# Two hybrid layers and two mixer layers on one core: the context keys of layers 0 and 1 are normalised in another order, their low parts are made by GpSimd, and the first query head is begun tile by tile

## The chip, the cores and the metric

The kernel runs on one core of a Trainium2 chip. The metric is the device time of one execution in microseconds (us); lower is better. The time before is the median of three runs.

## The reference, cut to what matters

Four layers follow each other on 512 positions of 1024 channels. The change lies in the first two (`l` = 0 and 1), in the latent attention of each:

```python
q = jnp.einsum("bsr,rk->bsk", rms_norm(q_lat, q_norm_g), w_uq)      # 384 -> 8 heads x (64 + 32)
q_nope, q_pe = jnp.split(q, [QK_NOPE], axis=-1)
q_pe = apply_rope(q_pe, cos, sin)
kv = jnp.einsum("bsr,rk->bsk", rms_norm(kv_lat, kv_norm_g), w_ukv)  # 256 -> 8 heads x (64 + 64)
k_nope, v = jnp.split(kv, [QK_NOPE], axis=-1)
```

`rms_norm(x, g)` is `x * rsqrt(mean(x*x) + eps) * g`. The latents `q_lat` (384 channels) and `kv_lat` (256 channels) and `k_rope` (32) are chunks of one projection of the layer's input. Causal attention over `qf`, `kf`, `v`, two convolution branches, a gated merge and a layer norm follow; then two more layers of another kind, which the change does not touch.

## The kernel before

**Numbers.** Every product of activations and weights is made of three matmuls: each operand is split into a high part (a rounded copy, `fp32r`) and a low part (the operand minus its high part), and `product` (L2034 to L2039) issues high x high (L2037), high x low (L2038) and low x high (L2039). A head of queries needs three tiles of 128 channels, so nine matmuls of 128x512; a chunk of the input projection needs eight tiles, so 24.

**Weights.** They come as blocks of 128x1024 through three slots. SyncE loads a block as soon as GpSimd has made the low part of the block three before it; ScalarE makes the high part (`split_to`, L483, or L480 for the two key and value blocks, which it also rearranges), for which the block must have landed and TensorE must have released the block three before it; GpSimd makes the low part in four pieces of 256 columns (`low_part`, L420, or `key_value_low`, L430). A chunk waits for the low part of each of its blocks. SyncE also loads pieces of `w_ada`, which VectorE multiplies up (`products`, L1239 and L1243).

**The stage around the change.** Block numbers here are those of layer 0; layer 1 has the same with 87 added. Blocks 6, 7 and 8 hold the query weights (24 tiles, three to a head), 9 and 10 the key and value weights, 11 is the first of the next stage. Block 10 takes the slot of block 7, which TensorE releases within head 5. Each engine runs its own program in order:

- TensorE: chunk of `k_rope`; sums of the squares of `kv_lat` by matmuls with ones (L2107); query heads 0 to 7 into four banks in turn; four key chunks (two heads each); four value chunks; then the first chunk of the next stage and the first attention scores. Head `h` from 4 on waits until ScalarE has taken (`qf`, L576) and VectorE has rotated head `h - 4`. The key chunks wait for the low parts `knL` of the normalised latent.
- VectorE: normalised query latent and its low parts (L1429, L1432, L1179); rotation of `k_rope`; for each head the rotation (L1448, L1449, L1451); behind head 1 the reciprocal of the key and value root (L1462) and the scaling of `kv_lat` (L1465, two tiles); behind head 3 the low parts `knL` (L1179, two tiles); behind every odd head a few `products`.
- ScalarE: high parts of the query latent (L606); high part of weight block 8; the root of the key and value sum (`kv_std`, L611); then per head the copy out of its bank (L576), with the high parts `knH` (L617) and the high part of block 9 behind head 2, block 10 behind head 5 and block 11 behind head 7; then eight copies of keys (L622) and four of values.
- GpSimd: low parts of the blocks in order: 8, then 9 and 10 (L430), then 11.

The lines that the change takes apart are these:

```python
pe.wait_ge(dve_done, Dn(l, "qnL", 2))           # TensorE, before head 0
pe.wait_ge(dve_done, Dn(l, "knL", 1))           # TensorE, before the first key chunk
```

Of the kernel before, what the change touches and what calls it, by code (L numbers as in the profile page):

```python
# [20 lines left out]
F32 = mybir.dt.float32  # L21
F32R = mybir.dt.float32r
I32 = mybir.dt.int32
ACT = mybir.ActivationFunctionType
ALU = mybir.AluOpType
# [4 lines left out]
S = 512  # L30
# [4 lines left out]
HEADS, NOPE, ROPE, VH = 8, 64, 32, 64  # L35
QL, KVL = 384, 256
# [19 lines left out]
POOL_PIECE = 256  # L56
RING = 3
Q_BANK = (4, 5, 0, 1)
# [55 lines left out]
def program(nc, io, known):  # L114

    ctx = ExitStack()
    with ctx:
# [8 lines left out]
        def sem(name):  # L126
            return ctx.enter_context(nc.semaphore(name))
# [18 lines left out]
        q_lat, kv_lat = at(R_L, [128, 3, S]), at(R_L + 3 * T, [128, 2, S])  # L146
        qnH, qnL = at(R_L + 5 * T, [128, 3, S], F32R), at(R_L + 8 * T, [128, 3, S], F32R)
        knH, knL = at(R_L + 11 * T, [128, 2, S], F32R), at(R_L + 13 * T, [128, 2, S], F32R)
# [7 lines left out]
        tmp = [at(R_T + T * i, [128, S]) for i in range(5)]  # L156
# [103 lines left out]
        s_park = nc.dram_tensor("s_park", [MH, 4, 128, SEQ], F32, kind="Internal").ap()  # L260
        ctx_landed, dft_landed, mask_landed = sem("ctx_landed"), sem("dft_landed"), sem("mask_landed")
        xm_parked, xc_parked = ([sem(f"{n}_parked{i}") for i in range(2)] for n in ("xm", "xc"))
        s_parked, xc_low = sem("s_parked"), sem("xc_low")
        xm_back, xc_back, s_back = sem("xm_back"), sem("xc_back"), sem("s_back")


# [51 lines left out]
        def B_UQ(l): return PER_LAYER * l + 6  # L318
# [93 lines left out]
        @block.gpsimd  # L412
        def _(pool):

            def low_part(b, slot):

                pool.wait_ge(weights_hi, b + 1)
                for i in range(0, BLK, POOL_PIECE):
                    part = slice(i, i + POOL_PIECE)
                    low = pool.tensor_tensor(w_lo[slot][:, part], w_raw[slot][:, part], w_hi[slot][:, part].bitcast(F32), ALU.subtract)  # L420
                low.then_inc(weights_lo, 1)

            def key_value_low(b):

                pool.wait_ge(weights_hi, b + 1)
                for n in range(4):
                    t, i = n // 2, 4 * (n % 2)
                    part = slice(POOL_PIECE * n, POOL_PIECE * (n + 1))
                    low, high = (w[b % RING][:, part].rearrange("p (h c) -> p h c", h=4) for w in (w_lo, w_hi))
                    low = pool.tensor_tensor(low, by_head(w_raw[b % RING])[:, i:i + 4, t, :], high.bitcast(F32), ALU.subtract)  # L430
                low.then_inc(weights_lo, 1)

            first = 0
            for l in range(L1):
                with pool.Fori(first, B_UKV(l) // RING) as i:
                    for r in range(RING):
                        low_part(i * RING + r, r)
                for b in UKV_BLOCKS[2 * l:2 * l + 2]:
                    key_value_low(b)
                low_part(b + 1, (b + 1) % RING)  # L440
                first = B_UKV(l) // RING + 1
            with pool.Fori(first, BASE_A // RING) as i:
                for r in range(RING):
                    low_part(i * RING + r, r)

            for b in range(BASE_A, BASE_B):
                low_part(b, b % RING)
                for h in range(MH):  # L450
                    for c in range(NC):
                        if b == ((AB["gates", 1] if h == 1 else AB["x", h, 3],) * 2 + (AB["q", h, 0], AB["q", h, 1]) if h else (AB["x", 1, 0], AB["x", 1, 1], AB["q", 0, 0], AB["q", 0, 1]))[c]:
                            pool.wait_ge(act_done, A("xcH", h, c))
                            for i in range(0, SEQ, POOL_PIECE):
                                part = slice(i, i + POOL_PIECE)
                                low = pool.tensor_tensor(xcL[:, c, part], c_acc[c % 2][:, part], xcH[:, c, part].bitcast(F32), ALU.subtract)  # L456
                            low.then_inc(xc_low, 1)
            with pool.Fori(BASE_B // RING, NBLOCKS // RING) as i:
                for r in range(RING):
                    low_part(i * RING + r, r)  # L460
# [3 lines left out]
        def _(act):  # L464
# [93 lines left out]
            for l in range(L1):  # L558
# [45 lines left out]
                for j in range(3):  # L604
                    act.wait_ge(dve_done, Dn(l, "qn", j))
                    act.activation(qnH[:, j, :], q_lat[:, j, :], ACT.Copy).then_inc(act_done, a(l, "qnH", j))  # L606

                act.wait_ge(pe_done, P(l, "k_rope"))
                split_to(B_KR(l) + 1 + RING)
                act.wait_ge(pe_done, P(l, "kv_sq", 1))  # L610
                act.activation(tmp[0][:], banks[2][:], ACT.Sqrt, bias=eps_rms[:], scale=1.0 / KVL).then_inc(act_done, a(l, "kv_std"))  # L611
                for h in range(HEADS):
                    evac(qf[0:NOPE, h, :], banks[Q_BANK[h % 4]][0:NOPE, :], (l, "q", h), None)
                    if h == 2:
                        for j in range(2):
                            act.wait_ge(dve_done, Dn(l, "kn", j))
                            act.activation(knH[:, j, :], kv_lat[:, j, :], ACT.Copy).then_inc(act_done, a(l, "knH", j))  # L617
                    if h in (2, 5, 7):
                        split_to(B_UQ(l) + RING + (h + 1) * 3 // 8)
                for h in range(HEADS):  # L620
                    act.wait_ge(pe_done, P(l, "k", h // 2))
                    act.activation(kf[0:NOPE, h, :], banks[KV_BANK[h // 2 % 2]][NOPE * (h % 2):NOPE * (h % 2 + 1), :], ACT.Copy)\  # L622
                        .then_inc(act_done, a(l, "k", h))
                for t in range(4):
                    evac(v_tok[:, t, :], banks[KV_BANK[t % 2]][:], (l, "v", t), None)
                split_to(B_UKV(l) + 2 + RING)
# [539 lines left out]
        def _(dve):  # L1166
# [4 lines left out]
            def wa(*label):  # L1171
                dve.wait_ge(act_done, A(*label))
# [4 lines left out]
            def low(dst, src, hi, *label):  # L1177

                dve.tensor_tensor(dst, src, hi.bitcast(F32), ALU.subtract).then_inc(dve_done, d(*label))  # L1179
# [199 lines left out]
            for l in range(L1):  # L1379
# [76 lines left out]
                for h in range(HEADS):  # L1456
                    wp(l, "q", h)
                    rotate(qf[64:96, h, :], banks[Q_BANK[h % 4]], l, "q_pe", h)
                    if h == 1:

                        wa(l, "kv_std")
                        dve.reciprocal(tmp[0][:], tmp[0][:]).then_inc(dve_done, d())  # L1462
                        wd()
                        for j in range(2):
                            dve.scalar_tensor_tensor(kv_lat[:, j, :], kv_lat[:, j, :], V("kv_norm_g", l, j), tmp[0][:],  # L1465
                                                     ALU.mult, ALU.mult).then_inc(dve_done, d(l, "kn", j))
                    if h == 3:
                        for j in range(2):
                            wa(l, "knH", j)
                            low(knL[:, j, :], kv_lat[:, j, :], knH[:, j, :], l, "knL", j)  # L1470
                    if h % 2:
                        products(B_UQ(l) + h // 2 + 1)
                for h in range(HEADS):
# [560 lines left out]
        def _(pe):  # L2034
            def product(out, wh, wl, xh, xl, start, stop):

                pe.matmul(out, wh, xh, start=start, stop=False)  # L2037
                pe.matmul(out, wh, xl, start=False, stop=False)  # L2038
                return pe.matmul(out, wl, xh, start=False, stop=stop)  # L2039

            def w_at(b, s):
                h, lo = w_hi[b % RING], w_lo[b % RING]
                return h[:, s * 128:(s + 1) * 128], lo[:, s * 128:(s + 1) * 128]
# [121 lines left out]
            for l in range(L1):  # L2165
# [21 lines left out]
                for j in range(2):  # L2187
                    pe.wait_ge(act_done, A(l, "kv_lat_sq", j))
                    sum_rows(banks[2], tmp[j % 2][:], 2, j, (l, "kv_sq", j))
                pe.wait_ge(dve_done, Dn(l, "qnL", 2))  # L2190
                for h in range(HEADS):

                    if h >= 4:
                        pe.wait_ge(act_done, A(l, "q", h - 4))
                        pe.wait_ge(dve_done, Dn(l, "q_pe", h - 4))
                    elif h == 2:
                        pe.wait_ge(act_done, A(l, "kv_lat", 1))
                    elif h == 3:
                        pe.wait_ge(dve_done, Dn(l, "k_rope"))
                    tiles = [(B_UQ(l) + (3 * h + k) // 8, (3 * h + k) % 8, qnH[:, k, :], qnL[:, k, :]) for k in range(3)]  # L2200
                    ends = [B_UQ(l) + i for i in range(3) if 3 * h <= 8 * i + 7 < 3 * h + 3]
                    chunk(banks[Q_BANK[h % 4]][:], tiles, (l, "q", h), ends)
                pe.wait_ge(dve_done, Dn(l, "knL", 1))
                b = B_UKV(l)
                for n in range(HEADS // 2):
                    if n == 0:
# [720 lines left out]
```

## Time and profile before

| | |
|---|---|
| median of three runs | 2390.27 us (2389.33 to 2391.31) |
| the profiled execution | 2394.42 us |
| its span, first to last instruction | 2392.6 us |
| granted TensorE clock, mean of the span | 0.978 of full speed |
| TensorE, VectorE, ScalarE, GpSimd busy | 95%, 62%, 36%, 45% of the span |

The span is cut into lines of one engine each. A timeline row reads: start, duration, engine, source line, what is written from what, count; a bracket behind it is the idle time of the engine before it and what ended that. Rows of a count above one are several instructions merged; their time is from the first start to the last end. The duration of a matmul row overlaps the next one; from start to start a 128x512 matmul takes 0.23 us where it lasts 0.39 us, and 0.43 us where it lasts 0.63 us.

### The profile page before, as it was taken

How to read it: one execution, taken by the hardware profiler on the slowest of the kernel's cores; microseconds unless marked ns; L12 is line 12 of the kernel's file. 1: busy time of each engine (PE TensorE's matmuls, PEld its weight loads, DVE VectorE, ACT ScalarE, POOL GpSimd, SP SyncE). 2: the span in 40 equal slices, each digit the busy share in tenths (PEclk: the TensorE clock that was granted, in tenths of full speed). 3: DMA queues.
4: the chain of work that ended last, by engine and by line, in shares of the span. 5: the costliest groups of instructions: out<-in, count | busy, mean ns of one | idle time of the engine just before them, and what ended most of it. 6: DMA issues, size and time to landing. Idle time of an engine off the chain costs nothing.

```text
span 2392.6 us, 29928 instructions
## 1 busy us (share of the span) xinstructions
PE 2265.2 (95%) x10750; PEld 1841.4 (77%) x10750; DVE 1487.8 (62%) x2352; ACT 849.9 (36%) x1383; POOL 1087.5 (45%) x1276
## 2 busy tenths in 40 slices
PE   6799999999989999999999999999999999899997
PEld 3588777888668877788868788877877877688886
DVE  5889956554578985755378666545765766433322
ACT  2343334222343333422254343334343444333321
POOL 1555436565345543666535444431344344333443
PEclk8999999999999999999999999999999999999999
DMA  8332224665143222355312223233234232122222
GB/s 302 119 119 80 71 65 143 210 204 161 54 144 111 71 71 62 132 165 159 116 53 97 75 98 110 70 103 120 80 123 141 80 124 84 53 72 74 74 75 76
DMA packets 93203, 259.80 MB, mean 109 GB/s; under 512 B 10128, under 2 KB 11536, under 8 KB 92944
## 3 DMA queue, kind: packets, MB, share of 16 engines
q1 hardware_dynamic: 71392, 210.23, 27.8%
q10 hardware_dynamic: 21680, 47.79, 5.6%
q8 instruction: 86, 1.41, 0.3%
q14 instruction: 45, 0.37, 0.0%
HBM read 237.01 MB, written 20.97 MB: 108 GB/s over the span
## 4 chain that ended last, share of the span: by engine, by line
PE 54%; issue 14%; POOL 12%; DVE 11%; ACT 3%; DMA 1%; ACTq 0%; POOLq 0%; DVEq 0%; SPq 0%
PE bank L2037 17%; PE bank L2038 17%; PE bank L2039 17%; POOL t L420 12%; DVE t L1735 2%; DVE t L1179 1%; PE bank L2107 1%; DVE t L1183 1%; PE bank L2415 1%; PE bank L2084 1%; POOL t L430 1%; DMA t<-blocks 0%; DVE t L1852 0%; PE bank L2126 0%; PE bank L2583 0%
## 5 line engine op out<-in xcount | busy, mean ns | idle before, releaser
L420 POOL TENSOR_TENSOR t<-t,t 128x256 fp32r<-128x256 f32 x1208 | 1031.2, 886 | 1194.5 <-ACT t L483 1194.3
L2037 PE MATMUL bank<-t,t 128*128 128x512 f32 (+1 forms) x3056 | 1177.8, 385 | 44.2 <-DVE t L1179 12.7
L2038 PE MATMUL bank<-t,t 128*128 128x512 f32 (+1 forms) x3056 | 1150.8, 377 | 0.0
L2039 PE MATMUL bank<-t,t 128*128 128x512 f32 (+1 forms) x3056 | 1148.3, 376 | 0.0
L2037 PEld LDWEIGHTS bank<-t,t 128*128 128x128 f32 x3056 | 582.5, 191 | 174.6 <-DVE t L1179 15.7
L2039 PEld LDWEIGHTS bank<-t,t 128*128 128x128 f32 x3056 | 581.0, 190 | 106.2
L2038 PEld LDWEIGHTS bank<-t,t 128*128 128x128 f32 x3056 | 582.4, 191 | 104.1 <-issue 4.5
L483 ACT ACTIVATE t<-t 128x1024 fp32r<-128x1024 f32 x302 | 317.0, 1054 | 296.3 <-PE bank L2039 243.5
L1243 DVE SCALAR_TENSOR_TENSOR t<-t,t,t 128x512 f32<-128x512 f32 x168 | 155.9, 947 | 104.1 <-DMA t<-w_ada 63.4
L1524 DVE SCALAR_TENSOR_TENSOR t<-t,t,t 128x512 f32<-128x512 f32 x240 | 210.3, 876 | 6.7
L1183 DVE SCALAR_TENSOR_TENSOR t<-t,bank 128x512 f32<-128x512 f32 x112 | 76.7, 685 | 159.6 <-ACT t L1136 60.4
L1179 DVE TENSOR_TENSOR t<-bank,t 128x256 fp32r<-128x256 f32 (+1 forms) x136 | 71.0, 558 | 121.4 <-ACT t L1116 63.5
L1735 DVE SCALAR_TENSOR_TENSOR t<-t,t,t 128x512 f32<-128x512 f32 (+1 forms) x160 | 142.2, 888 | 5.7
L640 ACT ACTIVATE t<-bank,t 128x128 f32<-128x128 f32 (+3 forms) x64 | 33.8, 529 | 137.8 <-DVE t L1497 137.6
L1187 DVE SCALAR_TENSOR_TENSOR t<-t,t 128x512 fp32r<-128x512 f32 x64 | 56.2, 888 | 35.4 <-ACT t L793 11.7
L742 ACT ACTIVATE t<-bank 128x512 f32<-128x512 f32 x48 | 28.5, 594 | 127.1 <-PE bank L2039 123.6
L456 POOL TENSOR_TENSOR t<-t,t 128x256 fp32r<-128x256 f32 x48 | 40.8, 881 | 68.0 <-ACT t L887 68.0
L1179 DVE TENSOR_TENSOR t<-t,t 128x512 fp32r<-128x512 f32 (+2 forms) x44 | 45.5, 1054 | 26.0 <-ACT t L866 17.6
L2244 PEld LDWEIGHTS bank<-t,t 128*128 128x128 f32 x320 | 46.0, 198 | 12.9 <-ACT t L650 9.3
L2107 PE MATMUL bank<-t,t 128*128 128x512 f32 x92 | 46.0, 640 | 8.3 <-ACT t L585 4.5
L1183 DVE SCALAR_TENSOR_TENSOR t<-t,t 128x512 f32<-128x512 f32 (+1 forms) x40 | 36.3, 907 | 22.8 <-ACT t L879 22.1
L2415 PE MATMUL bank<-t,t 128*128 128x512 f32 x96 | 37.4, 411 | 13.5 <-DVE t L1179 12.1
(248 smaller groups left out, 1742.8 us busy)
## 6 DMA issues: line engine op xcount, KB each, us to landing
t<-blocks SPq DMA_DIRECT2D x306, 512.0 KB, 3.7
t<-w_ada SPq DMA_DIRECT2D x144, 256.0 KB, 2.8
t<-w_ada SPq DMA_DIRECT2D x20, 512.0 KB, 11.6
xm_park<-t ACTq DMA_DIRECT2D x16, 384.0 KB, 2.3
s_park<-t ACTq DMA_DIRECT2D x16, 384.0 KB, 2.3
t<-xm_park ACTq DMA_DIRECT2D x16, 384.0 KB, 4.5
t<-s_park ACTq DMA_DIRECT2D x16, 384.0 KB, 5.3
xc_park<-t ACTq DMA_DIRECT2D x16, 256.0 KB, 2.1
```

Source lines behind the costliest of these rows:

```text
L420: low = pool.tensor_tensor(w_lo[slot][:, part], w_raw[slot][:, part], w_hi[slot][:, part].bitcast(F32), ALU.subtract)
L483: act.activation(w_hi[b % RING][:], w_raw[b % RING][:], ACT.Copy).then_inc(weights_hi, 1)
L1179: dve.tensor_tensor(dst, src, hi.bitcast(F32), ALU.subtract).then_inc(dve_done, d(*label))
L1183: dve.scalar_tensor_tensor(dst, tanh, 1.0, by, ALU.add, ALU.mult).then_inc(dve_done, d(*label))
L1243: dve.scalar_tensor_tensor(acc[:], src[:], c, acc[:], ALU.mult, ALU.add).then_inc(ada_sums, 1)
L1524: dve.scalar_tensor_tensor(a_acc[:, j, :], src, V("conv_a_w", l, j * TAPS_A + k), a_acc[:, j, :], ALU.mult, ALU.add).then_inc(dve_done, d( ...
L1735: dve.scalar_tensor_tensor(out, src, w(k), out, ALU.mult, ALU.add).then_inc(dve_done, d())
L2037: pe.matmul(out, wh, xh, start=start, stop=False)
L2038: pe.matmul(out, wh, xl, start=False, stop=False)
L2039: return pe.matmul(out, wl, xh, start=False, stop=stop)
L2107: pe.matmul(bank[:], ones[:], tile, start=(j == 0), stop=(j == n - 1)).then_inc(pe_done, p(*label))
L2415: pe.matmul(banks[7][:], w, lat[n], start=(first and n == 0), stop=(last and n == 1))
```

## The change

It touches layers 0 and 1 alike.

- ScalarE takes the root `kv_std` before the high part of block 8. `knH` moves from behind head 2 to behind head 3; the high part of block 9 stays behind head 2 and so now stands ahead of `knH`; the high part of block 11 moves from behind query head 7 to behind key head 3.
- VectorE takes the reciprocal and the scaling of `kv_lat` behind the rotation of head 0, not of head 1, and no longer makes `knL`.
- GpSimd makes `knL`, in four pieces of 128x256, behind the low parts of blocks 9 and 10. A semaphore `keys_low` counts them; TensorE waits for it before the first key chunk.
- TensorE begins head 0 by tile: it waits for each of the three low parts `qnL` in turn, not for the last of them first.

```diff
@@ gpsimd
                 for b in UKV_BLOCKS[2 * l:2 * l + 2]:
                     key_value_low(b)
+                for j in range(2):
+                    pool.wait_ge(act_done, A(l, "knH", j))
+                    for i in range(0, S, POOL_PIECE):
+                        part = slice(i, i + POOL_PIECE)
+                        low = pool.tensor_tensor(knL[:, j, part], kv_lat[:, j, part], knH[:, j, part].bitcast(F32), ALU.subtract)
+                    low.then_inc(keys_low, 1)
                 low_part(b + 1, (b + 1) % RING)
@@ scalar
+                act.wait_ge(pe_done, P(l, "kv_sq", 1))
+                act.activation(tmp[0][:], banks[2][:], ACT.Sqrt, bias=eps_rms[:], scale=1.0 / KVL).then_inc(act_done, a(l, "kv_std"))
                 act.wait_ge(pe_done, P(l, "k_rope"))
                 split_to(B_KR(l) + 1 + RING)
-                act.wait_ge(pe_done, P(l, "kv_sq", 1))
-                act.activation(tmp[0][:], banks[2][:], ACT.Sqrt, bias=eps_rms[:], scale=1.0 / KVL).then_inc(act_done, a(l, "kv_std"))
                 for h in range(HEADS):
                     evac(qf[0:NOPE, h, :], banks[Q_BANK[h % 4]][0:NOPE, :], (l, "q", h), None)
-                    if h == 2:
+                    if h == 3:
                         for j in range(2):
                             act.wait_ge(dve_done, Dn(l, "kn", j))
                             act.activation(knH[:, j, :], kv_lat[:, j, :], ACT.Copy).then_inc(act_done, a(l, "knH", j))
-                    if h in (2, 5, 7):
+                    if h in (2, 5):
                         split_to(B_UQ(l) + RING + (h + 1) * 3 // 8)
                 for h in range(HEADS):
                     act.wait_ge(pe_done, P(l, "k", h // 2))
...
+                    if h == 3:
+                        split_to(B_UQ(l) + RING + 3)
@@ vector
-                    if h == 1:
+                    if h == 0:
 
                         wa(l, "kv_std")
                         dve.reciprocal(tmp[0][:], tmp[0][:]).then_inc(dve_done, d())
...
-                    if h == 3:
-                        for j in range(2):
-                            wa(l, "knH", j)
-                            low(knL[:, j, :], kv_lat[:, j, :], knH[:, j, :], l, "knL", j)
@@ tensor
-                pe.wait_ge(dve_done, Dn(l, "qnL", 2))
-                for h in range(HEADS):
+                for k in range(3):
+                    pe.wait_ge(dve_done, Dn(l, "qnL", k))
+                    if k == 0:
+                        pe.wait_ge(weights_lo, B_UQ(l) + 1)
+                    mm = product(banks[Q_BANK[0]][:], *w_at(B_UQ(l), k), qnH[:, k, :], qnL[:, k, :], k == 0, k == 2)
+                mm.then_inc(pe_done, p(l, "q", 0))
+                for h in range(1, HEADS):
@@ tensor, before the key chunks
-                pe.wait_ge(dve_done, Dn(l, "knL", 1))
+                pe.wait_ge(keys_low, 2 * (l + 1))
```

## Rows read from the trace of the kernel before

**Rows 1.** The page: busy us of each engine, share of the span, instructions.
```profile
PE 2265.2 (95%) x10750; PEld 1841.4 (77%) x10750; DVE 1487.8 (62%) x2352; ACT 849.9 (36%) x1383; POOL 1087.5 (45%) x1276
```

**Rows 2.** Windows of layer 0: length, busy us per engine, granted clock, DMA.
```profile
105.00:113.00 8.00, 2.51 (x11) 1.73 (x10) 7.73 (x9) 3.75 (x7) 1.46 (x2) 0.84 0.16 50
113.00:121.00 8.00, 8.00 (x27) 6.42 (x28) 7.72 (x9) 3.06 (x5) 6.34 (x8) 0.73 0.23 84
```

**Rows 3.** Timeline of TensorE, layer 0: heads 5, 6 and 7, first key chunk.
```profile
105.12 0.47 PE L2037 MATMUL bank<-t,t 128*128 128x512 f32 x1
...
107.03 0.39 PE L2039 MATMUL bank<-t,t 128*128 128x512 f32 x1
112.91 0.77 PE L2037 MATMUL bank<-t,t 128*128 128x512 f32 x1 [5.49 <-ACT t L576]
...
118.95 0.39 PE L2039 MATMUL bank<-t,t 128*128 128x512 f32 x1
119.18 0.39 PE L2037 MATMUL bank<-t,t 128*128 128x512 f32 x1
```

**Rows 4.** Timeline of VectorE, layer 0.
```profile
101.72 1.06 DVE L1451 TENSOR_TENSOR t<-t,t 32x512 f32<-32x512 f32 x1
102.89 0.69 DVE L1448 TENSOR_TENSOR t<-bank,t 32x512 f32<-32x512 f32 x1
...
104.34 0.68 DVE L1451 TENSOR_TENSOR t<-t,t 32x512 f32<-32x512 f32 x1
105.05 3.35 DVE L1462 RECIPROCAL t<-t 128x512 f32<-128x512 f32 x1
108.44 1.41 DVE L1465 SCALAR_TENSOR_TENSOR t<-t,t,t 128x512 f32<-128x512 f32 x2
...
112.00 0.81 DVE L1451 TENSOR_TENSOR t<-t,t 32x512 f32<-32x512 f32 x1
...
115.35 2.24 DVE L1179 TENSOR_TENSOR t<-t,t 128x512 fp32r<-128x512 f32 x2
```

**Rows 5.** Timeline of ScalarE, layer 0.
```profile
98.91 1.06 ACT L483 ACTIVATE t<-t 128x1024 fp32r<-128x1024 f32 x1 [6.84 <-PE bank L2039]
...
109.22 1.29 ACT L617 ACTIVATE t<-t 128x512 fp32r<-128x512 f32 x2 [7.24 <-DVE t L1465]
...
112.80 1.05 ACT L480 ACTIVATE t<-t 128x1024 fp32r<-128x1024 f32 x1
117.12 0.59 ACT L576 ACTIVATE t<-bank 64x512 f32<-64x512 f32 x1 [3.28 <-PE bank L2039]
...
120.82 2.49 ACT L622 ACTIVATE t<-bank 64x512 f32<-64x512 f32 x4
```

**Rows 6.** Timeline of GpSimd, layer 0.
```profile
100.05 3.33 POOL L420 TENSOR_TENSOR t<-t,t 128x256 fp32r<-128x256 f32 x4 [7.26 <-ACT t L483]
111.54 7.80 POOL L430 TENSOR_TENSOR t<-t,t 128x256 fp32r<-128x256 f32 x8 [8.16 <-ACT t L480]
```

**Rows 7.** Timelines of layer 1: VectorE, GpSimd, TensorE (two rows).
```profile
695.70 3.35 DVE L1462 RECIPROCAL t<-t 128x512 f32<-128x512 f32 x1
702.19 7.80 POOL L430 TENSOR_TENSOR t<-t,t 128x256 fp32r<-128x256 f32 x8 [12.91 <-ACT t L480]
703.56 0.76 PE L2037 MATMUL bank<-t,t 128*128 128x512 f32 x1 [4.81 <-ACT t L576]
...
709.73 0.39 PE L2037 MATMUL bank<-t,t 128*128 128x512 f32 x1
```

**Rows 8.** TensorE elsewhere: first matmuls behind idle time.
```profile
256.74 0.66 PE L2263 MATMUL bank<-t,t 128*128 128x128 f32 x4 [3.82 <-DVE t L1509]
...
1324.05 0.80 PE L2037 MATMUL bank<-t,t 128*128 128x512 f32 x1 [4.41 <-POOL t L456]
...
1402.27 0.50 PE L2037 MATMUL bank<-t,t 128*128 128x512 f32 x1 [2.55 <-POOL t L420]
...
1482.62 0.78 PE L2415 MATMUL bank<-t,t 128*128 128x512 f32 x1 [2.13 <-DVE t L1179]
```

More of the change, by code:

```diff
@@ L262, in program @@
         xm_parked, xc_parked = ([sem(f"{n}_parked{i}") for i in range(2)] for n in ("xm", "xc"))
-        s_parked, xc_low = sem("s_parked"), sem("xc_low")
+        s_parked, xc_low, keys_low = sem("s_parked"), sem("xc_low"), sem("keys_low")
         xm_back, xc_back, s_back = sem("xm_back"), sem("xc_back"), sem("s_back")
```

## The prediction

> **What bounds the kernel now.** I read the page first: TensorE is busy for 95% of the span and no other engine passes 62% [rows 1], so an edit on another engine matters only where TensorE waits for it. Next, windows of 8 us over the query and key stage of layer 0 [rows 2]. In the first, TensorE works 2.51 of 8.00 us and VectorE 7.73: here VectorE is the bound. In the second, TensorE never stops but its granted clock is 0.73, so part of it runs at 1.2 instead of 2.4 GHz.
>
> The timeline of TensorE shows the hole: head 5 is 105.12 to 107.42, then 5.49 us of nothing, and head 6 begins at 112.91 [rows 3]. Head 6 needs its bank rotated by VectorE. VectorE went through the rotation of head 1 (102.89 to 105.02), the reciprocal (3.35), the scaling (1.41), a product, and the rotation of head 2, which ended at 112.81 [rows 4]. Head 6 then ran at the low clock: from its first matmul to ScalarE's copy of it 4.21 us passed (112.91 to 117.12) [rows 3, 5], where head 5 took 2.30 [rows 3]. So a head at the low clock costs 1.9 us more. Head 7 and the first key chunk follow without a hole; the chunk begins at 119.18 [rows 3]. GpSimd had run until 119.34 on the low parts of blocks 9 and 10 [rows 6], of which only block 10 is needed after the chunk's third matmul: TensorE and GpSimd arrive together. Layer 1 repeats it: VectorE's reciprocal at 695.70, a hole of 4.81 us, head 6 from 703.56, key chunk at 709.73, GpSimd done at 709.99 [rows 7].
>
> What the change is worth is therefore one number per layer: when does the first key chunk start, and at which clock.
>
> **The change part by part.** Layer 0 in full; times are on the axis of the rows.
>
> *Root ahead of block 8.* ScalarE sat 6.84 us before the high part of block 8 at 98.91 [rows 5], and the root was behind it. It now runs near 92.3. Nobody waited: VectorE had not reached the reciprocal. The move is what makes the next edit free of a wait; by itself it is worth 0. Bounds: a gain of 0, a loss of 0 (its 0.7 us fall into that idle time).
>
> *Reciprocal behind head 0.* The rotation of head 0 ends at 102.78 [rows 4]. Reciprocal and scaling take 3.35 + 1.41 and their gaps, 4.8 us, so `kv_lat` is normalised at 107.6 instead of 109.85. Then the rotation of head 1 takes 2.13 (102.89 to 105.02 in rows 4) and ends at 109.75. That is exactly when VectorE stood there before, so the rotation of head 2, and with it the earliest start of head 6, stays at 112.8. But head 5 waits for the rotation of head 1. It started at 105.12 and now starts at 109.85: **4.7 us later**. The hole in TensorE moves from between heads 5 and 6 to between heads 4 and 5; it is not closed (head 4 is done at about 105.2, so it is some 4.6 us wide).
>
> *What is queued behind head 5.* The high part of block 10 stands on ScalarE behind the copy of head 5. Before, head 5 was long done and this high part was at 112.80, held up by `knH` (109.22) [rows 5]. Now it waits for head 5 itself. If the hole drops the clock, head 5 takes 4.21 us, else 2.30. The trace has seven holes of 3.8 us or more, and behind each the low clock appears within a few matmuls (the two of this stage [rows 3, 7]; two more, of 3.82 and 4.41 us, stand in rows 8); of shorter ones some dropped it (2.13 us) and some not (2.55 us) [rows 8]. I take the low clock. Head 5 is then done at 109.85 + 4.21 = 114.06; the copy (0.59, overlapping 0.1) and the high part (1.05) [rows 5] end at 115.6.
>
> *Block 9 earlier.* Its high part, now ahead of `knH`, runs near 101.6 and its low part on GpSimd near 103.4 to 107.3, into a stretch where GpSimd was idle (8.16 us before 111.54) [rows 6]. That takes 3.9 us from GpSimd's later queue: half of the 7.80 [rows 6].
>
> *`knL` on GpSimd.* It stands behind block 10's low part. GpSimd begins block 10 at 115.7 and ends at 119.6 (3.9, half of 7.80). Then four pieces of 128x256, of the kind that took 3.33 for four [rows 6], but on VectorE 2.24 for both tiles [rows 4]: 119.6 + 3.3 = 122.9. TensorE starts the key chunk at 123.0. Before 119.18: **+3.8 us**. With head 5 at the high clock it would be 121.1, **+1.9**. The pieces were not in the old chain at all: VectorE had `knL` ready at 117.6, before TensorE needed it. VectorE's relief of 2.24 us per layer ends in idle time, since its next job that TensorE wants (rotations of heads 6 and 7, copies of the rotated key) has until the first score, far behind.
>
> *VectorE beside GpSimd.* The scaling took 1.41 with GpSimd idle; now GpSimd works on block 9 beside it. The nearest row is the last add of a rotation: 1.06 beside GpSimd against 0.68 without [rows 4, 6]. So 0 to 0.8 for two instructions; I take **+0.3**, which pushes head 5 and all behind it. The page SBUF — State Buffer of the Trainium skill (section "SBUF: two separate sides") says that VectorE with two SBUF inputs and GpSimd share one port pair by an exclusive lock, and the loser waits for the whole instruction. The 1.06 agrees in kind but is only 0.4 more. By that rule each of the two scalings could wait for a whole GpSimd piece; that is the last rival below.
>
> *Hole before the key chunk.* Heads 6 and 7 follow head 5 and are over by about 118.5 (head 7's bank is rotated just before 115.35, where `knL` stood on VectorE [rows 4]). The chunk starts at 123.0, a hole of 4.5 us; before there was none. By the holes counted above, nine or ten matmuls then run at the low clock: **+1.9 us** (4.21 - 2.30). If the clock stays up, the cost is 0 there, but then the high part of block 11, now in the middle of the key copies, shows: four key copies take 2.49 [rows 5], TensorE waits for them already, and 1.05 is put between; I estimate +0.5 for it. At the low clock TensorE is slower than ScalarE and it is hidden.
>
> *Head 0 by tile.* In layer 0 it starts near 92.1 instead of 93.98 and ends 1.3 us sooner, but head 4 still waits for the rotation of head 0 (102.78) [rows 4]. In layer 1 the sums of squares end after `qnL` is there. Worth 0 in both; bound of a gain: 1.3 us if nothing stood behind.
>
> *Block 11's high part later* costs nothing else: its low part is needed after four value chunks.
>
> Sum for layer 0: 3.8 + 0.3 + 1.9 = 6.0. Layer 1: the reciprocal starts at 693.45 (2.25 before 695.70), scaling ends at 698.25, head 1's rotation at 700.4, head 5 starts at 700.5 and is done at 704.7; copy and high part to 706.25, block 10's counterpart to 710.2, `knL` to 713.5, key chunk at 713.6 against 709.73 [rows 7]: 3.9 + 0.3 + 1.9 = 6.1. Both: **12.1 us**. Span 2392.6 + 12.1 = 2404.7, profiled execution 2394.42 + 12.1 = 2406.5. The profiled execution lies 4.15 above the median, so on the median's scale: 2390.27 + 12.1 = **2402.4 us**, 0.5% slower.
>
> **The rivals.** A change under 0.2% (4.8 us) is about what a measurement of this kernel can't tell from none.
>
> *The clock falls only in some of the four places.* Each is worth 1.9, and at head 5 both ways: head 5 at the high clock moves the chunk by only 1.9. One or two missing: 2397 to 2400.5. For it: the holes of 2.13 and 2.55 us went different ways [rows 8]. Against: mine are 3.9 to 4.6 wide. All four missing: 1.9 + 2.0 + 0.5 x 2 = 4.9, so 2395.2.
>
> *Not slower: the hole closes.* Head 5 now fills a part of the old hole, so head 6 begins behind only 1 us of idle time and runs at the high clock: 1.9 saved, head 7 over at 117.4, key chunk there if everything is ready: -1.8 per layer, 2386.7. It decides if `knL` is ready by 117.4, so block 10's high part by 110.2 (7.2 of GpSimd before it), so head 5 done by about 108.6. It can't begin before 109.85; 3.5 us are lacking. It needs that ScalarE or GpSimd do this work in another order than I read.
>
> *Given back later.* TensorE waits 3.82 us for VectorE at 256.74 [rows 8], and as much in layer 1. If VectorE, relieved, arrives there as early as before, the lateness is swallowed: 12.1 - 7.6 = 4.5, so 2394.8. Against: VectorE's chain there begins with the first score, which comes behind the key chunk and moves with it.
>
> *The port rule.* The two scalings each wait for a whole piece (3.9/4 = 0.98): 1.95 instead of 0.3, so +1.65 per layer: 2405.7.
>
> **How the numbers follow.** My forecast (low clock at all four places) 0.50; some missing 0.28; none 0.05; hole closed 0.06; given back 0.06; port rule 0.05. The range must leave out at most 0.2: 2394.8 (given back, and all four missing are inside) to 2405.7, which leaves out the closed hole, 0.06, and what I haven't thought of. The forecast's own range is 2400.5 to 2404.5. Slower by over 0.2% (above 2395.1): 0.50 + 0.28 + 0.05 and half of the none case, 0.86. Within 0.2%: the closed hole, the given back and the rest, less 0.03 for more gain than I see: 0.11. Faster: 0.03.
>
> **What would show it.** In the changed trace, layer 0: reciprocal at 102.8; head 4's end and head 5's start at 105.2 and 110; block 10's high part at 114.5 (112.7 at the high clock); GpSimd with one group of four near 103.4, then four more of block 10 and four of `knL` in one run that ends near 123; the wait before the first key chunk named GpSimd, 3.5 to 4.6 us, behind it 0.63 us matmuls. VectorE with no L1179 pair in 115 to 118. From the chunk on, the same trace shifted. The prediction is wrong if head 5 doesn't wait for head 1's rotation, if `knL` is over before head 7 is, or if the shift seen at 140 is gone at 300.

## The result, and the profile after

The changed kernel takes 2402.81 us (median of five runs, 2399.50 to 2405.09); the kernel before took 2391.31 in its five runs. The ratio is 1.0035 with a 95% interval of 1.0025 to 1.0046, which is 8.4 us (6.0 to 11.0) more. Run again beside the next three experiments, the same kernel gave 1.0055 (1.0041 to 1.0069), or 13.2 us (9.8 to 16.5). The forecast was 2402.4 and 12.1 us more: between the two, inside the second interval and a little above the first. Two executions far from all others are left out of the ratios: one of 2559.67 us (the kernel before, beside e1 to e4) and one of 7996.56 us (e10).

The page of the kernel after, its first part: TensorE's busy time is what it was [rows 1], in a longer span; GpSimd has eight more instructions and VectorE four fewer.

```profile
span 2397.7 us, 29932 instructions
PE 2263.2 (94%) x10750; PEld 1841.0 (77%) x10750; DVE 1484.0 (62%) x2348; ACT 850.6 (35%) x1383; POOL 1091.0 (46%) x1284
```

Windows of layer 0 (length, busy us of each engine, granted clock, DMA). Everything here lies some 1.5 us earlier than in the trace before, because this execution entered the layer sooner.

```profile
106.00:114.00 8.00, 5.45 (x17) 4.38 (x18) 7.50 (x12) 2.86 (x5) 0.00 (x0) 0.79 0.31 98
114.00:122.00 8.00, 3.30 (x14) 2.43 (x13) 7.57 (x10) 1.19 (x3) 7.08 (x8) 0.81 0.33 105
122.00:130.00 8.00, 7.48 (x25) 5.38 (x24) 7.70 (x15) 4.71 (x8) 1.38 (x2) 0.76 0.48 157
```

Before, one window of 8 us had little TensorE work [rows 2]; now two have, and the granted clock is 0.76 to 0.81 in all three. In the second, TensorE works 3.30 us and GpSimd 7.08.

TensorE, layer 0: heads 4, 5 and the first key chunk; the rows that answer to [rows 3].

```profile
103.41 0.40 PE L2043 MATMUL bank<-t,t 128*128 128x512 f32 x1
108.55 0.61 PE L2041 MATMUL bank<-t,t 128*128 128x512 f32 x1 [4.74 <-issue]
108.95 0.63 PE L2042 MATMUL bank<-t,t 128*128 128x512 f32 x1
...
116.13 0.39 PE L2043 MATMUL bank<-t,t 128*128 128x512 f32 x1
121.22 0.79 PE L2041 MATMUL bank<-t,t 128*128 128x512 f32 x1 [4.70 <-POOL t L444]
121.81 0.63 PE L2042 MATMUL bank<-t,t 128*128 128x512 f32 x1
```

Two holes stand where one stood. The first lies before head 5; the second is ended by L444, the new pieces of `knL`. Behind each, matmuls last 0.63 us: the lower clock, 1.2 GHz (granted clock 0.52 from 108.6 to 112.0 and 0.50 from 121.3 to 125.6).

VectorE, ScalarE and GpSimd in the same stretch; they answer to [rows 4], [rows 5] and [rows 6].

```profile
101.41 3.35 DVE L1470 RECIPROCAL t<-t 128x512 f32<-128x512 f32 x1
104.80 1.42 DVE L1473 SCALAR_TENSOR_TENSOR t<-t,t,t 128x512 f32<-128x512 f32 x2
106.31 0.69 DVE L1456 TENSOR_TENSOR t<-bank,t 32x512 f32<-32x512 f32 x1
...
107.76 0.68 DVE L1459 TENSOR_TENSOR t<-t,t 32x512 f32<-32x512 f32 x1
...
135.67 0.16 DVE L1483 MEMSET t<- 128x120 f32 x1 [4.89 <-PE bank L2043]
```

```profile
105.58 1.29 ACT L623 ACTIVATE t<-t 128x512 fp32r<-128x512 f32 x2 [3.96 <-DVE t L1473]
...
112.46 0.59 ACT L582 ACTIVATE t<-bank 64x512 f32<-64x512 f32 x1 [5.11 <-PE bank L2043]
112.96 1.05 ACT L486 ACTIVATE t<-t 128x1024 fp32r<-128x1024 f32 x1
```

```profile
101.93 2.81 POOL L430 TENSOR_TENSOR t<-t,t 128x256 fp32r<-128x256 f32 x4
114.08 3.46 POOL L430 TENSOR_TENSOR t<-t,t 128x256 fp32r<-128x256 f32 x4 [9.35 <-ACT t L486]
117.50 3.67 POOL L444 TENSOR_TENSOR t<-t,t 128x256 fp32r<-128x256 f32 x4
```

Read them as one chain. The rotation of head 1 ends at 108.44, head 5 begins at 108.55; ScalarE can copy it at 112.46 and make block 10's high part at 112.96; GpSimd begins at 114.08, having stood idle 9.35 us, and is through with `knL` at 121.17; the key chunk begins at 121.22. VectorE, relieved, later waits 4.89 us for TensorE: its time was not wanted.

Layer 1 does the same; TensorE and GpSimd, to be held against [rows 7].

```profile
702.87 0.77 PE L2041 MATMUL bank<-t,t 128*128 128x512 f32 x1 [4.42 <-issue]
715.55 0.79 PE L2041 MATMUL bank<-t,t 128*128 128x512 f32 x1 [4.80 <-POOL t L444]
```

```profile
708.32 3.55 POOL L430 TENSOR_TENSOR t<-t,t 128x256 fp32r<-128x256 f32 x4 [9.47 <-ACT t L486]
711.83 3.67 POOL L444 TENSOR_TENSOR t<-t,t 128x256 fp32r<-128x256 f32 x4
```

To be free of where an execution enters the layer, I measure the stage from the start of the low parts `qnL` on VectorE to the first attention score on TensorE. It took 45.0 us in layer 0 and 44.2 in layer 1 before (91.06 to 136.08, 682.47 to 726.63), and 51.2 and 50.6 after (89.64 to 140.85, 684.35 to 734.98): **+6.2 and +6.5**, together 12.7 us, against 6.0 and 6.1 forecast.

### The profile page after: what moved, and what is told of

Same layout as the page of the kernel before. It is cut to its first block, busy times and chain, and to the rows that moved or that the text cites. A ratio compares the mean times of both kernels' runs of the same rounds, so it can differ in the third digit from the quotient of the medians.

```text
span 2397.7 us, 29932 instructions
## 1 busy us (share of the span) xinstructions
PE 2263.2 (94%) x10750; PEld 1841.0 (77%) x10750; DVE 1484.0 (62%) x2348; ACT 850.6 (35%) x1383; POOL 1091.0 (46%) x1284
## 3 DMA queue, kind: packets, MB, share of 16 engines
q8 instruction: 86, 1.41, 0.2%
## 4 chain that ended last, share of the span: by engine, by line
PE 63%; DVE 14%; issue 11%; POOL 7%; ACT 3%; ACTq 0%; DMA 0%; POOLq 0%; DVEq 0%; SPq 0%
PE bank L2041 19%; PE bank L2042 19%; PE bank L2043 19%; POOL t L420 7%; DVE t L1739 2%; DVE t L1528 2%; DVE t L1187 1%; PE bank L2111 1%; DVE t L1191 1%; PE bank L2088 1%; PE bank L2424 1%; PE bank L2253 0%; PE bank L2244 0%; DVE t L1856 0%; PE bank L2130 0%
```

## The experiments

All times of the stage below are taken in that way, as differences to 45.0 and 44.2 us. Ratios are to the kernel before on the same chip. The column DMA is a wait of VectorE in layer 0, ahead of the rotation of head 0, for a piece of `w_ada` (1.36 us in the trace before); it varies between executions, no edit here touches its load, and where it is longer, the stage of layer 0 is longer by about as much.

| run | ratio (95%) | stage, layer 0 / 1 | DMA |
|---|---|---|---|
| the change, first profile | 1.0035 (1.0025 to 1.0046) | +6.2 / +6.5 | 1.38 |
| e1, the change again | 1.0055 (1.0041 to 1.0069) | +5.7 / +6.2 | 1.25 |
| e2, `knL` on VectorE | 1.0005 (0.9995 to 1.0014) | +0.5 / +0.3 | 1.66 |
| e3, reciprocal behind head 1 | 1.0009 (1.0000 to 1.0018) | +2.7 / +1.0 | 2.58 |
| e4, `knL` between blocks 9 and 10 | 1.0002 (0.9992 to 1.0011) | +2.1 / +0.7 | 3.18 |
| e5, holes overfilled | 1.0046 (1.0031 to 1.0061) | +5.5 / +6.3 | 1.44 |
| e6, kernel before, hole overfilled | 1.0014 (1.0005 to 1.0023) | +2.2 / +1.6 | 2.45 |
| e7, head 0 by tile alone | 0.9994 (0.9984 to 1.0003) | +2.3 / -0.4 | 3.26 |
| e8, root and reciprocal alone | 0.9997 (0.9988 to 1.0006) | -0.1 / 0.0 | 1.28 |
| e9, holes filled to size | 1.0020 (1.0010 to 1.0030) | +3.0 / +2.5 | 1.98 |
| e10, kernel before, hole filled to size | 0.9996 (0.9987 to 1.0005) | -1.2 / -1.4 | 1.30 |
| e11, between, and filled | 0.9990 (0.9979 to 1.0001) | -0.3 / -0.4 | 1.58 |

**e1, the change as it is**, a baseline for the next three.

> The changed kernel as it is, beside the others on the same chip. Both theories: 9 to 12 us above the kernel before, ratio 1.0035 to 1.005; head 5 of layer 0 begins 4.4 to 4.8 us behind head 4, the first key chunk behind idle time of 4.7 us with GpSimd's pieces of knL as its releaser.

The ratio came out above the expected span, the median difference (2402.80 against 2392.59, 10.2 us) inside it. In its trace the holes are 4.77 and 3.56 us in layer 0, 4.42 and 4.79 in layer 1. The 3.56 lies below the 4.7 expected: heads 5 and 6 ran longer at the low clock there and filled part of the hole. The key chunk begins where it does in the first profile, 31.55 us behind the start of `qnL` (31.58 there).

**e2, `knL` back on VectorE**, all else changed.

> The changed kernel with knL back on VectorE behind head 3; all else as changed. Theory (knL behind block 10 on GpSimd is the larger half): the first key chunk of each layer begins when block 10's low part is over, 3.6 us sooner, and without the long idle time its matmuls run at the high clock, 1.9 us more, less 0.5 for block 11's high part that then shows: -5 us per layer, so 0 to 3 us above the kernel before. Rival (the late head 5 is the whole cause, GpSimd's pieces are hidden by it): no more than 2 us below the changed kernel.

```diff
+                    if h == 3:
+                        for j in range(2):
+                            wa(l, "knH", j)
+                            low(knL[:, j, :], kv_lat[:, j, :], knH[:, j, :], l, "knL", j)
...
-                pe.wait_ge(keys_low, 2 * (l + 1))
+                pe.wait_ge(dve_done, Dn(l, "knL", 1))
```

The first key chunk of e2, its fourth and fifth matmul: the first three need only block 9, then TensorE waits 0.74 us for block 10, and the chunk runs at the high clock.

```profile
119.64 0.50 PE L2039 MATMUL bank<-t,t 128*128 128x512 f32 x1 [0.74 <-POOL t L430]
119.98 0.40 PE L2040 MATMUL bank<-t,t 128*128 128x512 f32 x1
```

The loss is gone with this one part, although head 5 is as late as in the change and runs at the low clock as there. The rival, the late head as the whole cause, falls.

**e3, reciprocal and scaling behind head 1 again**, `knL` still on GpSimd at the end of its queue.

> The changed kernel with the reciprocal and the scaling back behind head 1. Theory: head 5 no longer waits, so block 10's high part comes some 2 us sooner and the key chunk begins near where it did before (0.6 us later per layer), the hole stands before head 6 again and none before the key chunk: 1 to 4 us above the kernel before. Rival (knL on GpSimd costs by itself 3.7 us per layer whatever stands ahead of it): 7 us or more above.

```diff
-                    if h == 0:
+                    if h == 1:
                         wa(l, "kv_std")
```

```profile
105.59 0.47 PE L2041 MATMUL bank<-t,t 128*128 128x512 f32 x1 [0.25 <-issue]
113.26 0.77 PE L2041 MATMUL bank<-t,t 128*128 128x512 f32 x1 [5.37 <-issue]
```

These are heads 5 and 6 of layer 0: the hole is before head 6 again, and there is none before the key chunk. The loss shrinks to 0.1%. So GpSimd's pieces alone do not cost 3.7 us per layer, and the late head alone (e8) costs nothing: it takes both, in one queue.

**e4, the same pieces on GpSimd, in its idle time.**

> The changed kernel with knL on GpSimd between the low parts of blocks 9 and 10, where the trace shows GpSimd idle for 9.4 us. Theory (the place in GpSimd's queue costs, not the engine): the same as with knL on VectorE, 0 to 3 us above the kernel before. Rival (GpSimd is the wrong engine for it): 5 us or more above.

```diff
                 for b in UKV_BLOCKS[2 * l:2 * l + 2]:
                     key_value_low(b)
+                    if b == B_UKV(l):
+                        for j in range(2):
+                            pool.wait_ge(act_done, A(l, "knH", j))
...
```

GpSimd in layer 0 of e4: block 9, `knL` (L445), block 10.

```profile
101.92 3.23 POOL L430 TENSOR_TENSOR t<-t,t 128x256 fp32r<-128x256 f32 x4 [0.33 <-ACT t L487]
107.40 3.23 POOL L445 TENSOR_TENSOR t<-t,t 128x256 fp32r<-128x256 f32 x4 [2.25 <-ACT t L624]
115.97 3.52 POOL L430 TENSOR_TENSOR t<-t,t 128x256 fp32r<-128x256 f32 x4 [5.34 <-ACT t L487]
```

The pieces take 3.23 us there and nobody waits for them. The engine was not wrong; its place in the queue was.

**e8, the kernel before with the root ahead and the reciprocal behind head 0**, nothing else.

> The kernel before with the root ahead of block 8's high part and the reciprocal behind head 0; knL stays on VectorE, block 9's high part behind knH. Theory: the hole and its low clock move from head 6 to head 5, GpSimd ends block 10 about when it did (block 9 is over 1 us sooner than it was, block 10 waits for head 5): 0 to 1 us per layer. Rival (the late head 5 costs by itself what it is late, 4.7 us): 5 us or more above the kernel before.

No difference, in the whole and in the stage. The hole stands before head 5 (4.78 us in its layer 0), head 5 pays the low clock in place of head 6, and behind the third matmul of the key chunk TensorE waits 0.76 us for block 10 (0.77 in layer 1).

**e7, head 0 by tile alone.**

> The kernel before with head 0 begun by tile, nothing else. Theory: head 4 waits for the rotation of head 0 anyway, 0 us. Rival: up to 1.9 us less in layer 0.

No difference clear of the measurement. Of its +2.3 in layer 0, 1.9 is the longer wait for `w_ada`. VectorE in layer 0 of e7, that wait:

```profile
101.73 1.25 DVE L1243 SCALAR_TENSOR_TENSOR t<-t,t,t 128x512 f32<-128x512 f32 x1 [3.26 <-DMA t<-w_ada]
```

The interval does not exclude the rival's 1.9 us; the trace speaks against it, since TensorE stands idle for 3.76 us before head 4, which begins when head 0 is rotated.

**e5, the changed kernel with its holes filled.** Unused matmuls of ones keep TensorE busy; the kernel's results need none of them.

> The changed kernel with idle time of TensorE filled: eight matmuls of ones by 128x512, results unused, before head 5, and seven before the first key chunk, in layers 0 and 1. Nothing that another engine does is taken away. Theory (the holes cost twice, once as idle time and once as a low clock on head 5 and on the key chunk): head 5 and all behind it 1.9 us sooner, the key chunk at the high clock 1.9 more, less 0.5 for block 11's high part that then shows: 3.3 us per layer, so 4 to 8 us below the changed kernel. Rival (the low clock is not on the path, only the wait for knL is): within 1 us of the changed kernel.

```diff
+                    if h == 5:
+                        keep_busy(3, 8)
...
+                keep_busy(3, 7)
                 pe.wait_ge(keys_low, 2 * (l + 1))
```

A badly sized experiment: each such matmul is recorded as two of 0.44 us, so eight took 7.03 us in a hole of 4.7. The clock stayed up (granted 1.00 over the filling), but the filling itself then stood in the way: head 5 began 20.51 us behind the start of `qnL`, where the change has 18.91, and the time did not fall as expected.

**e9, the same with four and four.**

> The changed kernel with its holes filled by fewer matmuls: the run before showed that each takes 0.87 us (two passes), so that eight were 7.0 us and outlasted the hole of 4.7. Now four (3.5 us) before head 5 and four before the first key chunk. Theory: head 5 at the high clock and all behind it 1.9 us sooner, key chunk at the high clock 1.9 more, less 0.5: 3.3 us per layer, 4 to 8 us below the changed kernel, so 3 to 7 above the kernel before. Rival (the clock is not on the path): within 1 us of the changed kernel, 9 to 12 above the kernel before.

TensorE in layer 0 of e9: the filling before head 5, head 5, the filling before the key chunk, the chunk.

```profile
106.28 3.60 PE L2116 MATMUL bank<-t,t 128*128 128x512 f32 x8
109.78 0.47 PE L2041 MATMUL bank<-t,t 128*128 128x512 f32 x1
110.08 0.39 PE L2042 MATMUL bank<-t,t 128*128 128x512 f32 x1
...
117.28 3.59 PE L2116 MATMUL bank<-t,t 128*128 128x512 f32 x8
120.71 0.50 PE L2041 MATMUL bank<-t,t 128*128 128x512 f32 x1
121.05 0.40 PE L2042 MATMUL bank<-t,t 128*128 128x512 f32 x1
```

Matmuls behind both fillings last 0.4 us, not 0.63. The key chunk begins 1.2 us sooner in layer 0, which bears 0.6 us more of the `w_ada` wait, and 2.1 us sooner in layer 1; from the chunk to the first score it is 2.0 and 1.9 us less. The prediction had 1.9 for each. The stage is 3.2 and 4.0 us shorter than in the change, where 3.3 was expected, and the time 2397.45 against the kernel before at 2393.75, or +3.7. In the stages, 5.5 us are left of 12.7 (11.9 in e1): about half of the loss was the clock, the other half the waiting. VectorE's work and GpSimd's queue are as in the change.

**e6 and e10, the kernel before, filled.** Block 9's high part stands ahead of `knH` in both; ten matmuls before head 6 in e6, five in e10.

> The kernel before with two edits: the high part of block 9 ahead of knH (as in the change), and ten matmuls of ones, results unused, in the idle time before head 6. Theory: head 6 runs at the high clock, 1.9 us less, and the key chunk is ready by then because block 9's low part is over early: 1.5 to 1.9 us per layer, so 3 to 4 us below the kernel before, ratio 0.9983 to 0.9988. Rival (head 6's low clock is hidden by GpSimd or VectorE): no change.

> The kernel before with block 9's high part ahead of knH and five matmuls of ones (4.4 us) in the idle time before head 6, in place of ten (8.7 us), which outlasted it. Theory: head 6 at the high clock, key chunk 1 to 1.9 us sooner per layer: 2 to 4 us below the kernel before. Rival (GpSimd and VectorE hold the key chunk where it was): no change.

```diff
+                    if h == 6:
+                        keep_busy(3, 5)
```

e6 had e5's fault, 8.74 us of filling in a hole of 5.5, and was 0.14% slower instead of faster. In e10, head 6 begins at the high clock:

```profile
105.54 4.45 PE L2112 MATMUL bank<-t,t 128*128 128x512 f32 x10
111.06 0.47 PE L2037 MATMUL bank<-t,t 128*128 128x512 f32 x1 [1.06 <-issue]
111.36 0.39 PE L2038 MATMUL bank<-t,t 128*128 128x512 f32 x1
```

The stage is 1.2 and 1.4 us shorter, as the theory had it, but of that 2.6 us nothing is clear in the whole time (0.9996, 0.9987 to 1.0005). The profiled execution, 2385.17 us, was the shortest of its kernel, whose median is 2393.37. Why the gain doesn't show isn't settled: 2.6 us lie within what the interval allows.

**e11, `knL` between the blocks, four matmuls before head 5, block 11's high part where it was.**

> The changed kernel with knL on GpSimd between blocks 9 and 10, four matmuls of ones before head 5, and block 11's high part back behind query head 7. Theory: no hole but the one VectorE makes, no low clock, block 10's high part 1.9 us sooner: key chunk 1 to 1.5 us before where it was in the kernel before, 1 to 3 us below it. Rival: as the kernel before.

The lowest ratio of the series, 0.9990, with an interval that still touches 1: no version here is shown to beat the kernel before. The key chunk came 0.3 and 0.4 us sooner than in the kernel before (27.80 and 26.82 us behind the start of `qnL`), not 1 to 1.5, and in layer 0 head 4 ran in part at the low clock (granted 0.51).

## Why the prediction was right, point by point

*What bounds the stage* was read rightly: VectorE's chain sets head 6 before and head 5 after, and GpSimd's last piece sets the key chunk.

*The hole moves and does not close.* Forecast: head 5 4.6 us behind head 4. Measured 4.74, and 4.42 in layer 1; the rotation of head 2 stayed where it was (it ends 21.75 us behind the start of `qnL` in both traces), and head 6 follows head 5 without a gap, 0.8 us later than before. e8 shows that this part alone is free, as its expectation said from the prediction's terms.

*Low clock on head 5, head 0 by tile.* The low clock came in both layers. Head 5 took 3.91 us from first matmul to copy in layer 0 and 3.83 in layer 1, not 4.21, since the clock rose before it was over; in e1 it took 4.21 and 3.79. Head 0's earlier start only opened an idle time of 1.72 us before head 4, which went on waiting for the rotation of head 0: worth 0, as forecast.

*GpSimd's queue.* Forecast for block 10 and `knL` together: 7.2 us; measured 3.46 + 3.67 = 7.13, and 3.55 + 3.67 in layer 1. Key chunk against the start of `qnL`: 28.12 us before, 31.58 after in layer 0, so +3.5 where 3.8 + 0.3 was forecast; in layer 1 27.26 and 31.20, +3.9 where 4.2 was.

*VectorE beside GpSimd.* This term was wrong, for want of the meeting itself: GpSimd was through with block 9 at 104.74 and the scaling began at 104.80 (698.85 and 699.12 in layer 1), so it took 1.42 us, as without (1.41) [rows 4]: +0.0 instead of +0.3. I had given block 9 3.9 us; its four pieces took 2.81 beside the reciprocal, which reads one tensor, and 3.46 beside rotations. The last rival falls for the change with it, because the two never ran together. In layer 1 of e2, e4, e5 and e9 they met, over the last 0.3 us of a GpSimd piece: the scaling took 1.53 to 1.55 us there, 0.1 more. A meeting over a whole piece is in no trace. The shared port pair of the Trainium skill (SBUF — State Buffer, "SBUF: two separate sides") is neither confirmed nor refuted for the scaling; that GpSimd is faster beside the reciprocal agrees with it.

*Low clock on the key chunk.* Shown by the 0.63 us matmuls and by e9. Between the key chunk's start and the first score lie 2.7 us more than before in layer 0 (6.2 - 3.5) and 2.5 in layer 1, where 1.9 was forecast. In e9, at the high clock, the same stretch is still 0.7 and 0.6 us longer than before. That rest goes with block 11's high part among the key copies, which the prediction took for hidden at the low clock: in the change a wait of 0.52 us on a key copy stands before the first value chunk, and of 0.51 in layer 1. A wait of 0.49 to 0.56 us stands there in both layers of all seven traces that have block 11's high part among the key copies, at either clock, and in none of the other six, e11 among them. No run moved this copy alone.

*Nothing given back at 256.* The first wait for VectorE there is 3.83 us after and 3.82 before [rows 8]: the delay passes through whole, 4.8 us later on both sides of it. That rival falls too.

*The sum.* 12.7 us in the stages of the profiled executions, 11.9 in e1's, 12.1 forecast. That they lie so close is in part luck: up to the key chunk the change cost 0.6 and 0.3 us less than forecast, behind it 0.8 and 0.6 more. The rival with all four low clocks missing left out the 0.3 of each layer; by the prediction's own terms it is 5.5 us, not 4.9. In the whole time the change cost 8.4 and 13.2 us, with intervals of some 3 us on either side. The profiled execution of the changed kernel was the shortest of its five. Its end is only 5.1 us later than before while its layer 1 was 8.4 later. Part of that is in the third layer, which the change does not touch: an idle time of 4.41 us before 1324.05 [rows 8] is 2.86 us there, where e1 again has 4.42.

## What to carry to other kernels

A piece of work that goes to an idle engine inherits that engine's queue: put it where the engine stands idle (e4, no cost clear of the measurement), not behind a job that itself waits for TensorE (the change, 0.35 and 0.55%). Moving a long instruction of the bounding engine forward moves the hole that it makes; before doing so, ask what is queued behind the head that is now late. Two holes where there was one cost twice, as time and as clock.

## What the runs showed of the hardware

- The length of a hole alone does not tell whether the clock falls. Matmuls of 0.63 us follow idle times of 1.96 us (e2, before head 4 of layer 0, from the third matmul on), 2.31 us (e9, the same place, the first six matmuls, granted clock 0.50) and 3.76 us (e7, the same place, from the seventh on). None follow, up to the next hole, 1.72 us in the changed kernel, 2.55 us in the kernel before [rows 8], 3.12 us in e3 and 3.18 us in e4.
- Filling the holes with unused matmuls keeps the clock up: 0.39 to 0.40 us per 128x512 matmul after the first behind fillings of 3.6 and 4.45 us, where the same places had 0.63.
- An unused matmul of two fp32 operands of 128x128 and 128x512 is recorded as two of 0.44 us at the high clock (granted 1.00); eight of them took 7.03 us. Four that began at the low clock took 4.29 us (e11, layer 0), where four at the high clock took 3.6.
- Four GpSimd subtractions of 128x256 took from 2.79 us (e2, VectorE in its reciprocal) over 3.67 us (the change) to 4.62 us (e8, layer 1, VectorE in low parts, `products` and rotations).
